# One down part for both widths in the expert phase of a mixture-of-experts trunk (TensorE)

## What is computed

```python
probs = softmax(t @ router_w + router_b); top_p, top_i = top_k(probs, 2)
xs = t[tok]                                     # rows sorted by expert, 2048 in all
hid = silu(ragged_dot(xs, w1, sizes)) * ragged_dot(xs, w3, sizes)
y = ragged_dot(hid, w2, sizes) * top_p[...]     # w1, w3: 1024 x 3584, w2: 3584 x 1024 per expert
out = zeros.at[tok].add(y)
```

## Time and profile before

| | us |
|---|---|
| median of 3 runs | 5493.43 (5491.14 to 5495.01) |
| the profiled execution, its own time | 5488.2 |
| its span in the trace | 5486.3 |
| expert phase in that span | about 2907 to 5412 |

### The profile page before, as it was taken

How to read it: one execution, slowest core, us unless ns; L and a number is a source line. 1 busy time by engine, 2 the same in 40 slices (tenths; PEclk the granted TensorE clock), 3 DMA queues, 4 the chain that set the end, 5 groups by cost and what they waited for, 6 DMA issues and landing times. The chain is left out here.

```text
span 5486.3 us, 70996 instructions
## 1 busy us (share of the span) xinstructions
PE 5193.1 (95%) x29376; PEld 4413.3 (80%) x29377; DVE 2769.5 (50%) x2570; ACT 1811.3 (33%) x1615; POOL 760.3 (14%) x329
## 2 busy tenths in 40 slices
PE   7999999899999899999987999999999999999995
PEld 5777777688788677777757998989899899998985
DVE  7344267334425534423334454545665448854566
ACT  3123121222222212312223333333553336733354
POOL 1401111144444240111110000000000000000001
PEclk9999999999999999999998999999999999999997
DMA  5312134335536421211217555555785559965578
GB/s 180 101 42 68 39 96 113 111 97 146 161 96 175 151 85 39 69 39 51 77 70 242 191 185 192 176 177 191 242 301 192 177 191 333 356 200 180 188 250 309
DMA packets 812552, 860.96 MB, mean 157 GB/s; under 512 B 20018, under 2 KB 732850, under 8 KB 811826
## 3 DMA queue, kind: packets, MB, share of 16 engines
q1 hardware_dynamic: 804322, 826.35, 46.6%
q0 software_dynamic: 4608, 16.78, 0.8%
q10 hardware_dynamic: 3408, 14.68, 0.8%
HBM read 797.96 MB, written 57.67 MB: 156 GB/s over the span
## 5 line engine op out<-in xcount | busy, mean ns | idle before, releaser
L254 PE MATMUL banks<-e_x_hi,e_w_hi 128*128 128x256 f32 x3584 | 1023.8, 286 | 41.8 <-issue 32.1
L254 PE MATMUL banks<-h_hi,w_hi 128*128 128x512 f32 x2432 | 991.8, 408 | 50.6 <-DVE h_lo L735 23.9
L255 PE MATMUL banks<-e_x_lo,e_w_hi 128*128 128x256 f32 x3584 | 1023.0, 285 | 10.5 <-issue 10.5
L256 PE MATMUL banks<-e_x_hi,e_w_lo 128*128 128x256 f32 x3584 | 1022.1, 285 | 0.0
L256 PE MATMUL banks<-h_hi,w_lo 128*128 128x512 f32 x2432 | 955.2, 393 | 0.0
L255 PE MATMUL banks<-h_lo,w_hi 128*128 128x512 f32 x2432 | 954.3, 392 | 0.0
L2271 DVE TENSOR_TENSOR e_w_lo<-e_raw,e_w_hi 128x2048 fp32r<-128x2048 f32 x340 | 764.0, 2286 | 190.4 <-ACT e_w_hi L2209 190.4
L2209 ACT ACTIVATE e_w_hi<-e_raw 128x2048 fp32r<-128x2048 f32 x340 | 647.6, 1911 | 508.9 <-PE banks L256 499.5
L254 PEld LDWEIGHTS banks<-e_x_hi,e_w_hi 128*128 128x128 f32 x3584 | 696.0, 194 | 45.2 <-issue 34.2
L255 PEld LDWEIGHTS banks<-e_x_lo,e_w_hi 128*128 128x128 f32 x3584 | 695.7, 194 | 11.8 <-issue 11.8
L256 PEld LDWEIGHTS banks<-e_x_hi,e_w_lo 128*128 128x128 f32 x3584 | 695.7, 194 | 0.0
(11 more groups left out here) (307 smaller groups left out, 7117.9 us busy)
## 6 DMA issues: line engine op xcount, KB each, us to landing
e_raw<-in_moe_w_dram SPq DMA_DIRECT2D x510, 1024.0 KB, 6.0
w_raw<-in_ffn_w_dram SPq DMA_DIRECT2D x120, 512.0 KB, 3.9
w_raw<-in_w_in_dram SPq DMA_DIRECT2D x108, 512.0 KB, 4.0
f_ada_raw<-in_ada_w_dram SPq DMA_DIRECT2D x48, 512.0 KB, 5.0
g_ada_raw<-in_ada_w_dram SPq DMA_DIRECT2D x32, 512.0 KB, 4.1
e_io<-row_scratch SPq DMA_DIRECT2D x13, 1024.0 KB, 7.3
x_scratch<-x_res SPq DMA_DIRECT2D x24, 512.0 KB, 2.7
row_scratch<-stage SPq DMA_DIRECT2D x24, 512.0 KB, 2.6
```

Of the source, the lines that this page charges most:

```text
L254: pe.matmul(out, wh, rh, start=first, stop=False)
L255: pe.matmul(out, wh, rl, start=False, stop=False)
L256: return pe.matmul(out, wl, rh, start=False, stop=last)
```

## The change

The down part, `turn` and `between` stand once behind the choice of the up part. Inside each of the 14 chunks, the second row block's 12 matmuls stand first, under a condition of the program (`left > P`), and the first row block's 12 follow. Inside a chunk the order of the matmuls becomes: row block, then f, then column half.

```diff
-            def down(item, width):
+            def down_rows(c, t):
+                hi, lo = flat(w_hi[c % 4]), flat(w_lo[c % 4])
+                for f in range(2):
+                    hh = hid_hi[:, 2 * c + f, P * t:P * t + P]
+                    hl = hid_lo[:, 2 * c + f, P * t:P * t + P]
+                    for d in range(2):
+                        cols = slice(D * f + HALF * d, D * f + HALF * (d + 1))
+                        last = mm3(pe, m.ps[:, 4 + 2 * t + d, :], hh, hl, hi[:, cols], lo[:, cols],
+                                   c == 0 and f == 0, c == NF2 - 1 and f == 1)
+                return last
+
+            def down(item, left):
 
                 for c in range(NF2):
                     pe.wait_ge(s.lo2, NF2 * item + c + 3)
-                    hi, lo = flat(w_hi[c % 4]), flat(w_lo[c % 4])
-                    for f in range(2):
-                        for t in range(width // P):
-                            hh = hid_hi[:, 2 * c + f, P * t:P * t + P]
-                            hl = hid_lo[:, 2 * c + f, P * t:P * t + P]
-                            for d in range(2):
-                                cols = slice(D * f + HALF * d, D * f + HALF * (d + 1))
-                                last = mm3(pe, m.ps[:, 4 + 2 * t + d, :], hh, hl, hi[:, cols], lo[:, cols],
-                                           c == 0 and f == 0, c == NF2 - 1 and f == 1)
-                    last.then_inc(s.mm_done, 1)
+                    with pe.If(left > P):
+                        down_rows(c, 1)
+                    down_rows(c, 0).then_inc(s.mm_done, 1)
@@
                     with pe.If(left < P + 1):
                         up_narrow(item)
-                        turn(item + 2, 2 * NFG * item + (2 * NFG + 2))
-                        between(item)
-                        down(item, P)
                     with pe.Else():
                         up(item)
                         pe.sem_inc(s.hid_turned, 2 * NFG + 1)
-                        turn(item + 2, 2 * NFG * item + (2 * NFG + 2))
-                        between(item)
-                        down(item, ITEM)
+                    turn(item + 2, 2 * NFG * item + (2 * NFG + 2))
+                    between(item)
+                    down(item, left)
```

## The result

The changed kernel takes 5431.15 us (median of 4 runs, 5429.43 to 5433.23), the kernel before 5493.5 (4 runs): a ratio of 0.9886, 95% interval 0.9873 to 0.9898. A second set of runs gave 5431.12 us beside 5490.89 and 0.9892 (0.9875 to 0.9908). It is faster by 1.1%: 62.3 us in the first set, 59.8 in the second. All ratios are of fast executions; one execution of the kernel before, beside before_hoist, took 14609 us at a granted clock of 0.585 and is not in them.

A forecast was written before the change was run, and what follows sets the result against it. TensorE bounds the kernel, with matmuls in flight for 95% of the span, so only its idle time could pay. 5488.2 - 55.7 = 5432.5 us for the profiled execution, 5493.4 - 55.7 = 5437.7 for the median, said as 5437; range 5431 to 5448.

The forecast's parts named there:

- The mechanism: At wide items following wide ones, TensorE waits for program fetches; a smaller loop fetches nothing after its first pass.
- How much is kept: TensorE's program store keeps six to eight 16 KB packets; the changed loop needs seven with the one read ahead.
- first in, first out: The order in which TensorE's program store drops pieces, so a loop of nine misses every piece every time.
- two-page window: The Trainium skill's rule that a taken branch outside two cached pages forces a fetch, so back branches would always stall.
- What it removes: Stalls at five wide items following wide ones: 1258.2 us becomes five times 240.5, a gain of 55.7 us.
- The step from the profiled execution to the median: The profiled execution lies 5.2 us under the median, so the median goes from 5493.4 to 5437.7 us.
- What is late next: After an earlier start of wide items, the rests of u1 and u2 are in time by 1.4 and 2.8 us.
- Edits costed at nothing: First item, narrow items after wide ones, order inside a chunk and 14 branches an item: 0 us each.
- (a): The loop body is not kept and every piece is missed again; 25 to 37 us saved, 5456 to 5468; chance 0.07.
- (b): The new branches in the chunks are not covered by the sequencer's lead: 21 us more, 5458; chance 0.02.
- (c): Each condition in the chunks lets the instruction queue run dry: 134 us more, 5571; chance 0.03.
- (d): Some piece still falls out and the idle only moves, such as into the down part: 5484 to 5500; chance 0.04.

The follow-up runs named there:

- before_hoist: Kernel before with the 16 row transposes standing once and the down part still standing for each width behind a second choice: 5506.43 us, ratio 1.0018.
- before_shift: Kernel before with 80 identity transposes (160 instructions) put ahead of the item loop, the loop itself unchanged: 5434.3 us, ratio 0.9898.
- after_narrow_peel: Changed kernel with the last turn of the narrow up part written out, 209 instructions more: 5430.87 us in one run.
- before_shift70: Kernel before with 70 identity transposes put ahead of the item loop, the loop itself unchanged: 5432.1 us in one run.
- after_peel: Changed kernel with the last turn of the wide up part written out, nothing put ahead of the loop: 5460.67 us, ratio 0.9943.
- after_branches: Changed kernel with a second, always true condition around the first row block in each chunk, 168 more branches, none taken: 5430.81 us.
- before_again: Kernel before, unchanged, run again with a profile to see its spread: 5492.35 us over 11 runs, the profiled execution 5492.11.

## Why the prediction was right, and where it was not

- **The mechanism** was right, and each of its marks is there: 67 packets fewer were forecast and 68 came, 0.2 us a branch, full clock, no idle at the start. The size of the gain was too small, and the two points on it below say by which terms. The two shifts show that size and place together decide, with the doubled code left in.
- **How much is kept**: six to eight by the rows, and the forecast needed seven. before_shift and after_narrow_peel need eight by count and have no fetch, and the kernel before needs nine and has all. It is eight. The prediction's first in, first out fits all kernels but before_shift70, whose packets a ring fits. The Trainium skill's 128 KiB in blocks of 16 KiB ("Runtime: NRT & Kernel Launch", "Instruction fetch mechanics") agrees with it. Its two-page window does not: the changed loop jumps back over 5.3 pieces in 0.21 us.
- **What it removes**, the term of 55.7 us, was mis-sized: it should have been 59.8. It has two parts. The 240.5 us of an unstalled item is 240.2, 5 x 0.3 = 1.5 us in all: its first matmul starts 0.23 us after the start of the last one, which lasts 0.39, so they overlap by 0.16. (The range had 1 us for that.) And 1258.2 us was read from one execution. The three there are now have 1258.2, 1263.6 and 1260.7, mean 1260.8. With both the term is 1260.8 - 1201.0 = 59.8 us. By another cut, from its first matmul to its last, the expert phase took 2495.2, 2500.6 and 2497.1 us before and 2438.8 and 2438.5 after, 59.0 less.
- **The step from the profiled execution to the median** failed with it. I carried the gain over unchanged and took the 5.2 us by which the profiled execution lay under the median for an offset common to both kernels. It was not: the changed kernel's profiled execution lay 2.1 us over its median. Of the 5.2 us, 2.6 are the stalls, of which that execution had the least of the three; what the other 2.6 are stays open. So does the difference between the 59.8 of the stalls and the 62.3 of the first set; the second set has 59.8, and the medians of the kernel before lie between 5490.9 and 5493.8 in the four sets.
- **What is late next**: nothing, as forecast. The rest of u1 came at 3161.99 + 2.29 = 3164.28, 4.4 us after the start, and was wanted at 5.8.
- **Edits costed at nothing**: they held but for the narrow items, which took 127.7 us instead of 127.5, 0.7 us for the three behind wide ones. The first item started at 2917.25, again released by `e_w_lo`. The wait for `e_w_lo` at L254 grew from 9.6 us in 8 times to 13.6 in 10 by the 3.7 us that "issue" had there. The branches are covered.
- **The rivals**: (a) did not come, but its price was right. after_peel is that case, 29.5 us over the changed kernel at 5460.7, where (a) had 5456 to 5468, though its idles are 4.0 us on average and not 3.3. (b) and (c) fell by after_branches. (d) did not come either; an idle that moves into the down part is what before_hoist has.

## What to carry to other kernels

Where a loop of the program is long, look at the instruction queue's packets per pass before anything else. If they come in each pass, the idle at the jumps is a matter of how many pieces of 16 KB a pass touches, with the one read ahead. Count that number with the place of the loop head in its piece, and leave out pieces that are jumped over; one piece less gave everything here, and 33 instructions saved without a piece left every fetch. A gain that removes something random should be sized from several executions, not one.

## What was not expected of the hardware

- 160 needless instructions ahead of a loop made the kernel 1% faster (before_shift, 5434.3 against 5492.6 us).
- A slow fetch costs twice. In before_again the item of 254.2 us is 14.0 over the 240.2 of one without a stall. 9.5 us of that are idle. The other 4.5 are the clock: behind the two idles TensorE worked for 2.9 and for 5.9 us at a granted clock of 0.50. An idle of 1.6 us, as before wide items after narrow ones, left it at 1.00.
- A branch not taken took 65 to 80 ns and a taken one mostly about 210 (0.39 us at most in the changed kernel) on TensorE's sequencer when its target was there. When it was not, in three profiles of the kernel before, the back branch took 3.3 to 3.9 us and the jump over the narrow part 5.2 to 5.9, in the first item 6.4 to 6.6.
